# Sliding-window attention of a streaming-encoder block: probabilities turned through DRAM and VectorE in place of TensorE transposes

## What is computed

```python
def mixer_a(q, k, v, sinks, t5_bias):
    ...
    logits = jnp.einsum('bcqhgd,bckhd->bhgcqk', qc, kb) * SCALE
    logits = logits + bias[:, :, None]
    logits = jnp.where(valid[:, None, :], logits, NEG)
    p = jax.nn.softmax(jnp.concatenate([logits, sink], axis=-1), axis=-1)[..., :-1]
    out = jnp.einsum('bhgcqk,bckhd->bcqhgd', p, vb)
```

## Time and profile before

| | |
|---|---|
| median of 3 runs | 1044.88 us (1044.31 to 1045.07) |
| profiled execution | 1044.45 us |
| its span | 1042.6 us |
| TensorE busy | 1033.0 us, 99% |
| VectorE busy | 768.1 us, 74% |
| ScalarE busy | 473.8 us, 45% |
| GpSimd busy | 212.6 us, 20% |
| granted TensorE clock, mean | 0.999 |

### The profile page before, as it was taken

The page is one execution under the profiler, slowest core; times in us unless marked ns, Lnnn a source line. Parts: engine busy times, 40 slices in busy tenths (PEclk is TensorE's granted clock), DMA queues, the critical chain, the costliest instruction groups (busy, mean ns, idle before and its releaser), DMA issues.

```text
span 1042.6 us, 15884 instructions
## 1 busy us (share of the span) xinstructions
PE 1033.0 (99%) x5599; PEld 858.8 (82%) x5599; DVE 768.1 (74%) x1513; ACT 473.8 (45%) x972; POOL 212.6 (20%) x200
## 2 busy tenths in 40 slices
PE   9999999999999999999999999999999999999997
PEld 8899888787877888888888888888888888888886
DVE  5853478767679568889988878786444777788997
ACT  6533256555469466856221131131344444444562
POOL 0400000000000003039677576572100000000000
PEclk9999999999999999999999999999999999999999
DMA  9460111111052375135543444436777733454344
GB/s 249 120 208 9 47 50 38 47 47 41 27 142 111 81 212 149 55 111 184 201 172 142 154 150 162 160 133 217 240 242 250 236 98 101 132 192 144 99 136 168
DMA packets 98958, 142.15 MB, mean 136 GB/s; under 512 B 33448, under 2 KB 50736, under 8 KB 96832
## 3 DMA queue, kind: packets, MB, share of 16 engines
q1 hardware_dynamic: 98192, 140.94, 42.1%
q10 hardware_dynamic: 688, 0.20, 0.1%
HBM read 100.77 MB, written 44.60 MB: 139 GB/s over the span
## 4 chain that ended last, share of the span: by engine, by line
PE 90%; DVE 5%; issue 2%; ACT 2%; DMA 1%; POOL 0%; DVEq 0%; SPq 0%; ACTq 0%
PE ps L2053 26%; PE ps L2055 26%; PE ps L2054 26%; PE ps L2262 2%; PE ps L2248 2%; PE ps L2229 2%; PE ps L2177 1%; DVE wc_lo L1745 1%; PE ps L2208 1%; PE ps L2190 1%; DVE b_lo L1734 1%; PE ps L2065 1%; DMA up_raw<-in_w_up 1%; DMA xraw<-in_x 0%; DVE b_raw L1703 0%
## 5 line engine op out<-in xcount | busy, mean ns | idle before, releaser
L2053 PE MATMUL ps<-b_hi,wc_hi 128*128 128x512 f32 x448 | 174.8, 390 | 0.1
L2054 PE MATMUL ps<-tm_lo,sm_hi 128*128 128x512 f32 (+1 forms) x450 | 174.6, 388 | 0.0
L2055 PE MATMUL ps<-tm_hi,sm_lo 128*128 128x512 f32 (+1 forms) x450 | 174.6, 388 | 0.0
L2053 PE MATMUL ps<-tm_hi,sm_hi 128*128 128x512 f32 (+1 forms) x450 | 174.6, 388 | 0.0
L2054 PE MATMUL ps<-b_lo,wc_hi 128*128 128x512 f32 x448 | 174.4, 389 | 0.0
L2055 PE MATMUL ps<-b_hi,wc_lo 128*128 128x512 f32 x448 | 174.3, 389 | 0.0
L1347 ACT ACTIVATE sm_hi<-sm_raw 128x512 fp32r<-128x512 f32 x112 | 70.7, 631 | 162.1 <-DMA sm_raw<-u_matrices 162.1
L1962 DVE TENSOR_TENSOR sm_lo<-sm_raw,sm_hi 128x512 fp32r<-128x512 f32 x112 | 77.7, 694 | 77.9 <-ACT sm_hi L1347 77.4
L2053 PEld LDWEIGHTS ps<-b_hi,wc_hi 128*128 128x128 f32 x448 | 84.1, 188 | 18.5 <-DVE wc_lo L1745 1.0
L2054 PEld LDWEIGHTS ps<-tm_lo,sm_hi 128*128 128x128 f32 x450 | 84.5, 188 | 17.5
L2053 PEld LDWEIGHTS ps<-tm_hi,sm_hi 128*128 128x128 f32 x450 | 84.5, 188 | 17.4
(11 more groups left out here) (233 smaller groups left out, 2078.5 us busy)
## 6 DMA issues: line engine op xcount, KB each, us to landing
u_matrices<-stage SPq DMA_DIRECT2D x112, 256.0 KB, 2.0
sm_raw<-u_matrices SPq DMA_DIRECT2D x112, 256.0 KB, 2.6
up_raw<-in_w_up SPq DMA_DIRECT2D x16, 1024.0 KB, 5.0
w<-in_w_down SPq DMA_DIRECT2D x64, 256.0 KB, 3.7
w_raw<-in_w_in SPq DMA_DIRECT2D x8, 512.0 KB, 3.5
xr<-in_x SPq DMA_DIRECT2D x8, 512.0 KB, 4.7
x_rows<-xr SPq DMA_DIRECT2D x8, 512.0 KB, 4.9
xf<-x_rows SPq DMA_DIRECT2D x8, 512.0 KB, 3.6
```

The costliest lines, as they stand in the source:

```text
L2053: pe.matmul(out, w_hi_, x_hi_, start=start, stop=False)
L2054: pe.matmul(out, w_hi_, x_lo_, start=False, stop=False)
L2055: return pe.matmul(out, w_lo_, x_hi_, start=False, stop=stop)
```

## The change

For eleven rounds (0 to 7, 9, 11 and 13) the TensorE transposes and the ScalarE copy are left out. SyncE stores the round's probabilities to DRAM, waits for them to land, and loads them back with four DMAs, one for each 32 partitions, so that the 32x32 blocks lie in transposed places; VectorE then transposes within the blocks (`turn_a`), straight into `probT_a`. Rounds from 5 on alternate between the two `prob_a` buffers. `weigh_a` waits for VectorE's count, and reads the heads in another order.

```diff
+AHEAD = 5
+
+TURNED_FIRST = {2: 0, 4: 1, 6: 2, 8: 3, 14: 5}
+TURNED_LAST = {10: 4, 14: 6}
+TURNED_A = (0, 1, 2, 3, 4, 5, 6, 7, 9, 11, 13)
...
         def first_probs(r):
-            return prob_a[turn(r)]
+            return prob_a[r % 2 if r >= AHEAD else 0]
...
+            def exchange_probs(r):
+
+                if r not in TURNED_A:
+                    return
+                m = turned_a(r)
+                sp.wait_ge(s_p, 4 * r + 4)
+                sp.dma_start(p_dram[m], first_probs(r).rearrange("p h n -> p (h n)")).then_inc(s_hst, 16)
+                sp.wait_ge(s_hst, 48 + 16 * (m + 1))
+                rows = p_dram[m].rearrange("(c j) (h a i) -> a j h c i", c=4, a=4, i=32)
+                for a in range(4):
+                    sp.dma_start(first_probs(r)[32 * a:32 * a + 32].rearrange("j h (c i) -> j h c i", c=4), rows[a]
+                                 ).then_inc(s_hb[m % 2], 16)
...
+                for r in ((0, 1, 2), (3, 4), ())[g]:
+                    exchange_probs(r)
             load_fill(1)
+            exchange_probs(5)
             load_fill(2)
+            exchange_probs(6)
+            exchange_probs(7)
             load_fill(3)
...
+            def turn_a(r):
+
+                if r not in TURNED_A:
+                    return
+                m = turned_a(r)
+                dve.wait_ge(s_hb[m % 2], 80 + 64 * (m // 2 + 1))
+                if r >= 2:
+                    dve.wait_ge(s_pv, 2 * r - 2)
+                nc.vector.transpose(probT_a[r % 2].rearrange("p h n -> p (h n)"),
+                                    first_probs(r).rearrange("p h n -> p (h n)")).then_inc(s_ptd, 1)
...
-                if r:
-                    dve.wait_ge(s_pt, r if r <= T else r - 1)
+                former = r - 1 if r < AHEAD else -1 if r == AHEAD else r - 2
+                if former in TURNED_A:
+                    dve.wait_ge(s_ptd, turned_a(former) + 1)
+                elif former >= 0:
+                    dve.wait_ge(s_pt, chunks_until(2 * former + 2))
...
+                if n in TURNED_FIRST:
+                    turn_a(TURNED_FIRST[n])
                 normalize_a(n)
...
+                if n in TURNED_LAST:
+                    turn_a(TURNED_LAST[n])
...
             def transposes_a(n):
+                if n // 2 in TURNED_A:
+                    return
...
-                pe.wait_ge(s_pta, copies(n + 1, True))
+                if r in TURNED_A:
+                    pe.wait_ge(s_ptd, turned_a(r) + 1)
+                else:
+                    pe.wait_ge(s_pta, copies(n + 1, True))
```

More of the change, by code:

```diff
@@ L177, in chunks_of @@
     if n < A_STEPS:
-        return [(0, 4, True)] if n % 2 else []
+        return [(0, 4, True)] if n % 2 and n // 2 not in TURNED_A else []
     if paired(n) and nk <= 2:
@@ L216, in copied, with turned_a @@
     by_act = chunks_of(n)[c][2]
-    return sum(d[2] == by_act for m in range(n) for d in chunks_of(m)) + sum(d[2] == by_act for d in chunks_of(n)[:c + 1])
+    return (0 if by_act else len(TURNED_A)) + sum(d[2] == by_act for m in range(n) for d in chunks_of(m)) + sum(d[2] == by_act for d in chunks_of(n)[:c + 1])
 def copies(n, by_act):
-    return sum(c[2] == by_act for m in range(n + 1) for c in chunks_of(m))
+    return (0 if by_act else len(TURNED_A)) + sum(c[2] == by_act for m in range(n + 1) for c in chunks_of(m))
 CHUNK_BANKS = chunk_banks()
+def turned_a(r):
+    return sum(m < r for m in TURNED_A)
 def t5_runs():
@@ L470, in build @@
         h_dram = nc.dram_tensor("h2_row_tiles", (TURNED, P, D), F32).ap()
+        p_dram = nc.dram_tensor("prob_round_tiles", (len(TURNED_A), P, 4 * P), F32).ap()
         s_const = sem("const_landed")
@@ L488, in build @@
         s_xlo = sem("x_lo_ready")
-        s_w1 = [sem(f"first_weights_landed_then_h2_rows_stored_or_blocks_landed{n}") for n in range(3)]
+        s_w1 = [sem(f"first_weights_landed_then_rows_stored_or_blocks_landed{n}") for n in range(3)]
         s_w1hi = sem("first_weights_hi_ready")
@@ L541, in build @@
         s_hst, s_hb = s_w1[0], s_w1[1:3]
+        hst0 = 48 + 16 * len(TURNED_A)
+        hb0 = [80 + 64 * sum(m % 2 == n for m in range(len(TURNED_A))) for n in range(2)]
         s_t2 = sem("h2_transposed")
@@ L718, in _ @@
             load_bias(4)
+            for r in range(8, 10):
+                exchange_probs(r)
             load_fill(4)
+            for r in range(10, 2 * T):
+                exchange_probs(r)
             load_fill(5)
@@ L759, in _ @@
                         sp.dma_start(h_dram[pos], hs[:, s]).then_inc(s_hst, 16)
-                        sp.wait_ge(s_hst, 48 + 16 * (pos + 1))
+                        sp.wait_ge(s_hst, hst0 + 16 * (pos + 1))
                         rows = h_dram[pos].rearrange("(c j) (k a i) -> a j k c i", c=4, a=4, i=32)
@@ L1084, in _ @@
                         exp(m, hh)
-                if n:
+                if n and chunks_of(n - 1):
                     copy_chunk(n - 1, 0)
@@ L1098, in _ @@
                         exp(m, hh)
-                    if m == n + 1:
+                    if m == n + 1 and chunks_of(n - 1):
                         copy_chunk(n - 1, 0)
@@ L1103, in _ @@
                 splits(n)
-                copy_chunk(n + 1, 0)
+                if chunks_of(n + 1):
+                    copy_chunk(n + 1, 0)
                 for m in (n + 1, n + 2):
@@ L1624, in _ @@
                 take_low(halves_done(n - 1))
+                if n == 2 * T:
+                    turn_a(T - 1)
                 normalize_a(n)
                 take(halves_done(n))
+                if n > 2 * T:
+                    turn_a(n // 2 - 1)
                 normalize_a(n + 2)
@@ L1688, in turn_blocks @@
                 s = pos % 2
-                dve.wait_ge(s_hb[s], 80 + 64 * (pos // 2 + 1))
+                dve.wait_ge(s_hb[s], hb0[s] + 64 * (pos // 2 + 1))
                 raws = sum(ORDER[i] < 4 for i in range(pos))
@@ L2180, in transposes_a @@
             def transposes_a(n):
+                if n // 2 in TURNED_A:
+                    return
                 bank, former = CHUNK_BANKS[n + 1, 0]
-                if n == 0:
-                    pe.wait_ge(s_vst, 2)
-                elif former is not None:
+                if former is not None:
                     pe.wait_ge(s_pta, copied(*former))
@@ L2205, in weigh_a @@
                     for hh in range(2):
+                        heads = slice(hh, 4, 2) if r in TURNED_A else slice(2 * hh, 2 * hh + 2)
                         cols = slice(64 * hh, 64 * hh + 64)
                         out_ = ps[cols, 7, :].rearrange("p (q i n) -> p q i n", q=2, i=2)[:, (r + 1) % 2, :, 64 * half:64 * half + 64]
-                        last = pe.matmul(out_, values[:, cols], probT_a[r % 2][:, 2 * hh:2 * hh + 2, 64 * half:64 * half + 64],
+                        last = pe.matmul(out_, values[:, cols], probT_a[r % 2][:, heads, 64 * half:64 * half + 64],
                                          start=True, stop=True)
```

## The result

The changed kernel took **1046.95 us** (median of 8 runs, 1046.16 to 1049.66) against 1044.78 for the kernel before (8 runs beside it); the ratio is 1.0026, 95% interval 1.0017 to 1.0035. So it is slower by about a quarter of a per cent. Forecast were 1046.7, and 1041.0 to 1050.0. The profiled execution took 1046.47 us, with a span of 1044.7: 2.1 more than the span of before.

What follows compares the result with a forecast made beforehand. TensorE, busy 99% of the span, was taken to bound the kernel. Transposes saved, -4.84 us, and waits of 4.6, 1.4 and 0.6 summed to +1.8: 1046.7 us for the median, range 1041.0 to 1050.0.

Steps and rivals of the forecast that it cites:

- What is taken out: Four TensorE transposes in each of 11 rounds, 0.44 us a round by the chain: 4.84 us less.
- The exchange and the transpose: Per round, store and four loads take 6.5 us (5.5 to 7.3), then VectorE's block transpose 0.65 us.
- Round 0: TensorE, at round 0's values at 80.4, waits 4.6 us for blocks loaded at 84.3 and turned at 85.0.
- the store stands behind them: Round 0's store, issued at 71.5, lands at 79.9, behind the replicated bias rows and v_odd transfers.
- The rival's argument: For a store not held up: bias rows need not hold all 16 DMA engines; 1040.0 us, chance 0.17.
- half 3's bank: After round 0's values and three fills, TensorE waits 1.4 us until VectorE gives this bank back at 88.4.
- the 0.6 at half 5: TensorE wants half 5's bank at 95.4, VectorE has taken it at 96.0: a wait of 0.6 us.
- The clock rival: TensorE's clock falls during round 0's wait, adding 0.6 to 1.6 us: 1047.3 to 1048.3; chance 0.2.
- The sum: Transposes saved and three waits: -4.84 + 4.6 + 1.4 + 0.6 = +1.8 us; from -0.4 to +6.
- Rounds 1 to 4: One probability buffer chains these rounds, ready at 86.7, 95.5, 104.4, 113.2; fill tile 1's weights, issued at 119.4, cost nothing.
- What would show it: Profile signs: TensorE idle some 4.6 us before 85, VectorE idle from 74 to 84, a second gap of 1.4.
- the signs against: Fast side: store before 75 or blocks before 80. Slow side: clock under 1.00 behind 84, or gap near 127.

Runs made afterwards that it cites:

- ten rounds: The change, but with round 0 back on TensorE's transposes and ScalarE's copy: 1039.97 us, ratio 0.9957.
- six: The change, but only rounds 5, 6, 7, 9, 11 and 13 turned by VectorE, the others left on TensorE: 1041.54 us, ratio 0.9973.
- the run with both edits: The change, with halves 3 and 5 taken before the waits for blocks, and 36 overwritten TensorE matmuls before round 0's values: 1046.31 us, ratio 1.0020.
- the dummy matmuls: The change, with 36 TensorE matmuls, their result overwritten, before the wait for round 0's transpose: 1047.38 us, ratio 1.0032.
- the rows in pieces: The change, with the 3 MB of replicated bias rows issued in eight pieces, one behind each exchange of rounds 0 to 7: 1040.36 us, ratio 0.9960.
- both sets of rows walked row by row: The change, with the 3 MB of replicated bias rows and the first group's 1.5 MB walked row by row, not head by head: 1041.31 us.

## Why the prediction was right, point by point

- **What is taken out**: 0.44 us a round, by the chain's piece. Measured: 0.45 (ten rounds), 0.48 (six), 0.37 (eleven). The row of the chain decided rightly. By the 390 ns, in bf16, of the Trainium skill (VectorE: DVE Perf Modes, The three transpose paths), the ten rounds would have been worth 16 us, an estimate from that page; the runs do not agree.
- **The exchange and the transpose**: 6.5 and 0.65 us; round 1's took 6.65 and 0.71.
- **Round 0**: store out at 71.5, landing 79.9, blocks 84.3, wait 4.6; measured 71.49, 79.52, 84.08, 4.27. The times are right, the reason half: "the store stands behind them" is no matter of order in the queue. The rows hold 8 of the 16 engines whichever queue they come from. The rival's argument, that the rows "need not hold all of them", is true and no help: the store needs them all.
- **The step that went otherwise**: "Then it does the values (0.6) and three fills (1.4), is at 87.0, and needs half 3's bank [...]: 1.4 us more", and with it the 0.6 at half 5. TensorE did not stand idle for these 2.0 us. It worked from 84.88 to 88.94 at the lower clock, which cost 2.03, came to half 3's bank at 88.49, when it had been free since 88.09, and was idle 0.07 at half 5's. With the clock held up the two waits are there, as 1.05 and 0.56.
- **Why the time is right all the same**: what sets it is when VectorE has taken half 5, 96.0 by the forecast and 95.92 measured, and no work of TensorE lies on the way there. The forecast had this chain right. How TensorE spent the time until then, standing or working slowly, made no difference. That the slow work fitted so nearly into the waits, with 0.07 to spare, is luck.
- **The clock rival** (chance 0.2) took place in the clock and not in the time: it asked for 0.6 to 1.6 more than the sum, and nothing on top of it shows at 95.97. It had counted slow work behind half 3's bank as lost, and left out that the wait of 0.6 at half 5 would take up the first 0.6 of it. The Trainium skill's rule named there (TensorE: Matmul & The Clock Gate) agrees with this run: behind a wait for a transfer TensorE ran at 0.51.
- **The sum**: up to half 5's bank the forecast lost 6.6 us in waits, and the change lost 4.27 + 0.25 (late start) + 2.03 + 0.07 = 6.6. In all +1.8 was forecast and +2.1 measured in the profiled execution. The difference is the 0.29 for the late scaling of a tile at 141.56, in a stretch for which no gap was forecast.
- **Rounds 1 to 4**: 86.7, 95.5, 104.4 and 113.2 forecast, 86.4, 95.4, 105.7 and 114.5 measured; fill tile 1's weights went out at 120.5 instead of 119.4. They cost next to nothing here: round 4's transpose, which waits behind their split, ended at 128.09, and round 4's values began at 128.15 without a counted gap. In the run with both edits the same place cost 1.0.
- **What would show it**: idle time, releaser and VectorE's long wait as forecast; the gap of 1.4 is missing. Of the signs against, the granted clock under 1.00 behind 84 is there, but without the longer time that it was to stand for.

## What to carry to other kernels

Price work that leaves a saturated engine by its piece in the chain, then look for the first user that has to wait for the way round: here ten of eleven rounds gained 0.45 us each, and one gave it all back. A transfer on the path waits for whatever its DMA engines still hold, so read the DMA share: here 0.50 for a long copy meant that half of the engines carried it, at 187 GB/s, against 323 GB/s with all of them. And where two delays lie over each other, as the slow clock and the bank waits did, taking away one of them gains little: look for the chain that sets the end of both.

## What the runs showed of the hardware

- A copy with an outer loop of 8 kept 8 of 16 DMA engines (share 0.50), with 7 it kept 7 (0.44); with 128 the share went to 0.97.
- Kernels in which TensorE waits for round 0's store scatter widely: the change 1046.2 to 1049.7, with the dummy matmuls 1046.0 to 1051.1. Three without that wait stay together: 1039.6 to 1040.1 with ten rounds, 1041.2 to 1041.8 with six, 1039.8 to 1040.6 with the rows in pieces. But with both sets of rows walked row by row, where the profile shows no such wait either, five runs go from 1039.3 to 1042.2. The landing of this one store, 79.25 to 80.56 in the profiles of the seven kernels with these rows in front, may be a part of it; that it is the cause is not shown.
